# State-space pairs one turn later, and an out-projection that begins with the attention rows

## The chip, the cores and the metric

The kernel runs on one core of a Trainium2 chip. The metric is the device time of one execution in microseconds (us); the kernel before takes 3050.3 us (median of 3 runs, 3049.33 to 3051.59). The engines named here are TensorE (PE; PEld is its weight load), VectorE (DVE), ScalarE (ACT), GpSimd (POOL) and SyncE (SP), whose queue issues nearly all loads.

## The reference

One layer of a hybrid decoder over 512 prompt tokens and 8 sequences of 8 new tokens (576 columns). One projection feeds a sparse-attention group of 8 heads and a state-space (Mamba-2) group of 16 heads. Their outputs stand side by side and go through one output projection:

```python
u = rmsnorm(x, norm_attn)
proj = u @ w_in
q, k, v, qi, ki, wi, z, xbc, dtr = jnp.split(proj, _split_points(), axis=-1)
att = att_fn(q, k, v, qi, wi, ki)
y, h_fin = ssd_scan(xs, dt, A, Bm, Cm, h0, chunk)
y = (y + d_skip.astype(jnp.float32)[:, None] * xs.astype(jnp.float32)).astype(x.dtype)
y = rmsnorm(y.reshape(B, T, SSM_WIDTH) * jax.nn.silu(z), ssm_norm)
h = x + jnp.concatenate([att, y], axis=-1) @ w_out
f = rmsnorm(h, norm_ffn)
h = h + (jax.nn.silu(f @ w_gate) * (f @ w_up)) @ w_down
```

Two facts matter. The norm over `y` needs all 16 state-space heads, so no `y` row can be used before the last pair of heads has added its squares. The attention rows need no such norm.

## The kernel before, in words

Every large product is done in split precision: a weight block is cast to a high part (ACT, `WH`), the rest is its low part (POOL, `WL`), and TensorE adds three products, high by high, high by low, low by high. A half unit (`half_unit`, L802) is 8 input rows of 128, each 6 matmuls of 288 columns. Two half units make one output tile of 128 rows by 576 columns; inside the turns each half unit is called a product, numbered 0 to 5 (q, q, k, k, v, v of one head). Its raw weights come in halves (`load_half`, L480, tile `raw3`), three buffers deep.

After the conv stage come nine turns (`turn_pe`, `turn_act`, `turn_dve`, `turn_sp`). Turn i holds, interleaved by hand on every engine:

- `units`: products 0 to 5 of head i (turns 0 to 7). In turn 0 products 0 to 3 run first, in a row.
- `att`: the attention of head i - 1 (turns 1 to 8): logits of the prompt (L968), cached keys transposed (L987) and multiplied (L997), softmax, values (L1188), cached values (L1165), and a last transpose (L1169) before head i - 1 is stored to the DRAM tensor `mixS`.
- `mamba`: the state-space pair i (turns 0 to 7): transposes of x and B (L977), C by B (L1066), states per chunk (L1079), old states transposed (L1006), outputs per chunk (L1014, L1017), outputs of the new tokens (L1025), state update (L1175). Its inputs are eleven loads (`load_mamba`, L508 to L516), the last of them the old states `h0`. All of it waits on one semaphore, `ssm_in`. `load_mamba(i + 1)` goes out in turn i, after the states of pair i are stored (`hout`), because it overwrites the same tiles.

A PSUM bank of the turns is handed on by a count (`nth`), so the number of uses of each bank per turn is part of the program.

After turn 7 the squares of all pairs are summed (L1199), ACT takes the root (L1586), DVE the reciprocal (L2170). Turn 8 has only the attention of head 7. Then comes the output projection: 16 units over 16 rows of `mixS` that are loaded one by one into six buffers (`load_mix`, L607), the `y` rows scaled by DVE (`y_norm`, L2179), cast by ACT (L1611, `AH`), and their low part made by DVE (L2184, `AL`). Unit 0 takes each row as its low part is ready, in the order y rows 0 to 7 (rows 8 to 15 of `mixS`), then attention rows 0 to 7; the 15 units behind it find all rows in place. On SP, the first weights of `w_out` and the rows stand behind waits, the first being for `hout` of the last pair: the weights' buffer overlaps `h0`.

Of the kernel before, what the change touches and what calls it, by code (L numbers as in the profile page):

```python
# [13 lines left out]
P = 128  # L14
# [22 lines left out]
def build(nc, I, O):  # L37
    ctx = ExitStack()
    with ctx:
# [257 lines left out]
        MAMBA = {"xtok0", "xtok1", "btok0", "btok1", "cb0", "cb1", "su", "hTb0", "hTb1", "y0", "y1", "y2", "y3", "ys", "us0", "us1", "fin"}  # L297
        where = dict(turn)
        in_turn, in_mamba, in_att = {}, {}, {}
        n_all, n_mamba, n_att = [0] * 4, [0] * 4, [0] * 4  # L300
        for name, b in turn:
            in_turn[name] = n_all[b]
            n_all[b] += 1
            if name in MAMBA:
                in_mamba[name] = n_mamba[b]
                n_mamba[b] += 1
            else:
                in_att[name] = n_att[b]
                n_att[b] += 1

        def nth(name, i):

            b = where[name]
            if isinstance(i, int) and i == 0:
                return first[b] + in_mamba[name]
            if isinstance(i, int) and i == 8:
                return first[b] + n_mamba[b] + 7 * n_all[b] + extra[b] + in_att[name]
            return n_all[b] * i + (first[b] + n_mamba[b] - n_all[b] + in_turn[name])


        first, extra = list(count), [0, 0, 1, 1]
        for b in range(4):
            count[b] = first[b] + n_mamba[b] + 7 * n_all[b]
        plan("ssy0", 2)
        plan("ssy1", 3)
        for b in range(4):
            count[b] += n_att[b]
# [66 lines left out]
        def _(sp):  # L394
# [179 lines left out]
            turn_sp(7, mamba=False, more=False)  # L574
# [19 lines left out]
            def out_cols(q):  # L594

                def src(dst):
                    d = dst.rearrange("p (k c) -> p k c", c=256)
                    return [(d[:, 8 * h:8 * h + 8, :], wo_v[:, 8 - 8 * h:16 - 8 * h, 256 * q:256 * q + 256]) for h in range(2)]
                return src

            def load_mix(j):
# [205 lines left out]
        def _(pe):  # L807
# [201 lines left out]
            def y_chunk(i, c):  # L1009

                tclaim(pe, f"y{c}", i)
                pe.wait_ge(s["mt_done"], 10 * i + 2 * c + 2)
                for e in range(2):
                    last = mm(bank(f"y{c}")[e * DS:(e + 1) * DS, 0:P], xtok[:, c, e * DS:(e + 1) * DS], mt[:, (2 * c + e) % 4, :], start=True, stop=True)  # L1014
                if c:
                    pe.wait_ge(s["hT_done"], 4 * i + c)
# [3 lines left out]
            def y_decode(i):  # L1020
                tclaim(pe, "ys", i)
                pe.wait_ge(s["mt_done"], 10 * i + 10)
# [7 lines left out]
            def turn_pe(i, att=True, units=True, mamba=True):  # L1030
                a = i - 1
                early = isinstance(i, int) and i == 0
# [4 lines left out]
                if units:  # L1037
                    product(i, 0)
                    if early:
# [5 lines left out]
                        pe.wait_ge(s["h_init"], 4)  # L1045
# [8 lines left out]
                if mamba:  # L1054
                    pe.wait_ge(s["ssm_in"], LOADS * (i + 1))
# [17 lines left out]
                if mamba:  # L1073
                    tclaim(pe, "su", i)
                    pe.wait_ge(s["xw_done"], i + 1)
# [50 lines left out]
                def rest():  # L1126
# [13 lines left out]
                    if mamba:  # L1140
                        tclaim(pe, "fin", i)
                        pe.wait_ge(s["hT_done"], 4 * i + 4)
# [28 lines left out]
            def update(i, g):  # L1171

                tclaim(pe, f"us{g}", i)
                pe.wait_ge(s["bblk"], i + 1)
# [25 lines left out]
            turn_pe(8, units=False, mamba=False)  # L1200
# [81 lines left out]
        def _(act):  # L1282
# [171 lines left out]
            def exp_decay(i, n):  # L1454
                act.wait_ge(s["seg"], 10 * i + n + 1)
# [15 lines left out]
            def turn_act(i, att=True, units=True, mamba=True, nxt=True):  # L1471
                a = i - 1
                later = not (isinstance(i, int) and i == 0)
                latera = not (isinstance(i, int) and i <= 1)
                early = not later
# [7 lines left out]
                if mamba:  # L1483
                    act.wait_ge(s["ssm_in"], LOADS * (i + 1))
# [4 lines left out]
                    if later:  # L1489
                        act.wait_ge(s["xw_done"], i)  # L1490
# [6 lines left out]
                if mamba:  # L1497
                    if later:
                        act.wait_ge(s["bblk"], i)
# [44 lines left out]
                if att:  # L1544
# [3 lines left out]
                    for t in range(4):  # L1548
# [4 lines left out]
                        if t == 2 and mamba:  # L1553
                            if later:
                                act.wait_ge(s["finout"], 16 * i)
                            evac(i, "fin", fin, bank("fin")[:, 0:P])
                if mamba:
                    if not att:
                        if later:
                            act.wait_ge(s["finout"], 16 * i)  # L1560
                        evac(i, "fin", fin, bank("fin")[:, 0:P])
                    tgiven(act, "fin", i)
                    act.dma_start(bass.AP(O["ssm_prompt"].tensor, i * (P * P), [[P, P], [1, P]]), fin).then_inc(s["finout"], 16)
                    act.wait_ge(s["y_done"], i + 1)
                    act.dma_start(bass.AP(mixS.tensor, i * (P * NT) + 8 * P * NT, [[NT, P], [1, NT]]), xs[:, :]).then_inc(s["ymix"], 16)
                if att:
                    exp_logits(i, 4)
                if mamba:
                    act.wait_ge(s["h_done"], 2 * i + 2)
                    act.dma_start(bass.AP(O["ssm_sample"].tensor, i * (P * P), [[P, P], [NM * DS * P, NB], [1, P]]), h0[:, :, :]).then_inc(s["hout"], 16)  # L1570
# [8 lines left out]
            turn_act(0, att=False)  # L1579
# [3 lines left out]
            turn_act(7, nxt=False)  # L1583
            for h in range(2):
                wait(act, f"ssy{h}")
                taken(actv(rstd[:, h, :], bank(f"ssy{h}")[:, 0:HALF], ACT.Sqrt, bias=eps[:, :], scale=1.0 / (NM * DS)), f"ssy{h}")  # L1586
            turn_act(8, units=False, mamba=False)
# [854 lines left out]
```

## Time and profile before

| | |
|---|---|
| median of the runs | 3050.3 us (3049.33 to 3051.59) |
| profiled execution | 3047.6 us, of which the profiled span is 3045.6 us |
| TensorE busy | 2827.9 us (93%) |
| VectorE, ScalarE, GpSimd busy | 1509.6, 952.2, 548.0 us |
| mean granted TensorE clock | 0.965 of full |
| HBM traffic | 116 GB/s over the span |
| turn 0, from product 0 to 3 done to turn 1 | 540.4 to 597.0 us |
| turns 1 to 7 | 597.0 to 1150.9 us |
| turn 8 and the start of the output projection | 1150.9 to 1212.85 us |

Busy shares are averages over stages. Times of events are in us from the start of the span. The number in brackets at the end of a row of a timeline is how long the engine had been idle before it, and what ended that.

### The profile page before, as it was taken

Reading aid. Unit: us, or ns where it says so; the run is one execution under the profiler, and the core shown is the slowest. Engines: PE = TensorE matmul, PEld = TensorE weight load, DVE = VectorE, ACT = ScalarE, POOL = GpSimd, SP = SyncE. Lnnn points to the kernel's source line nnn. Section 1 sums busy time; section 2 is a strip of 40 time slices with the busy share of each in tenths; the row PEclk is TensorE's granted clock in tenths of the full one; section 3 lists DMA queues with packets and bytes.
Section 4 is the critical chain, followed back from the end, with each engine's and each line's share of the span. In section 5 each row is a group of like instructions: output and inputs, shape, how many; then the busy total and the mean of one; then the engine's idle time right before and its main releaser. Section 6 shows DMA issues by size and latency. Waiting matters only on the chain.

```text
span 3045.6 us, 49651 instructions
## 1 busy us (share of the span) xinstructions
PE 2827.9 (93%) x20713; PEld 2688.3 (88%) x20713; DVE 1509.6 (50%) x2311; ACT 952.2 (31%) x1442; POOL 548.0 (18%) x230
## 2 busy tenths in 40 slices
PE   6999999689999996997799999999999999999997
PEld 5887898577777773997799999999999999999997
DVE  3312599444444443213767667676766733222323
ACT  4223222133333322323443434334343322121222
POOL 1222233111111110332000000000000033333331
PEclk8999999799999997998899999999999999999999
DMA  6422231455555545433123233332323352323221
GB/s 201 119 67 77 68 106 50 126 145 145 152 148 152 151 139 169 140 127 104 64 94 124 99 119 100 108 112 97 127 99 107 127 198 99 114 99 115 99 99 63
DMA packets 367372, 354.00 MB, mean 116 GB/s; under 512 B 40957, under 2 KB 321125, under 8 KB 365880
## 3 DMA queue, kind: packets, MB, share of 16 engines
q1 hardware_dynamic: 334136, 325.20, 33.7%
q10 hardware_dynamic: 33024, 25.77, 2.6%
q8 instruction: 158, 2.59, 0.3%
q14 instruction: 54, 0.44, 0.0%
HBM read 303.18 MB, written 49.13 MB: 116 GB/s over the span
## 4 chain that ended last, share of the span: by engine, by line
PE 57%; issue 32%; POOL 7%; DVE 2%; ACTq 1%; ACT 1%; POOLq 0%; DVEq 0%
PE PS L1242 32%; PE PS L1224 18%; PE PS L802 6%; POOL WL L705 4%; POOL WL L734 3%; ACTq L1286 0%; DVE XR L2282 0%; ACTq L1287 0%; DVE xo_t L2287 0%; DVE xo_x L2287 0%; DVE y_out L2357 0%; POOL WL L726 0%; ACT WRAW L1295 0%; DVE rstd L2275 0%; PE PS L817 0%
## 5 line engine op out<-in xcount | busy, mean ns | idle before, releaser
L802 PE MATMUL PS<-AH,WH 128*128 128x288 f32 (+1 forms) x2208 | 493.5, 306 | 21.0 <-DVE AL L2184 7.3
L1224 PE MATMUL PS<-H,WH 128*128 128x288 f32 x2816 | 489.5, 296 | 0.7 <-DVE us L2249 0.7
L802 PE MATMUL PS<-AL,WH 128*128 128x288 f32 (+1 forms) x2208 | 481.1, 300 | 0.0
L802 PE MATMUL PS<-AH,WL 128*128 128x288 f32 (+1 forms) x2208 | 480.1, 299 | 0.0
L724 POOL TENSOR_TENSOR WL<-WRAW,WH 128x1024 fp32r<-128x1024 f32 x88 | 213.8, 2430 | 1378.8 <-ACT WH L717 1378.8
L1224 PEld LDWEIGHTS PS<-H,WH 128*128 128x128 f32 x2816 | 414.4, 189 | 0.9 <-issue 0.9
L802 PEld LDWEIGHTS PS<-AH,WH 128*128 128x128 f32 (+1 forms) x2208 | 363.6, 193 | 44.9 <-issue 28.9
L1242 PE MATMUL PS<-xo_t,WH 128*128 128x288 f32 x1888 | 380.1, 296 | 8.6 <-ACT kept L1643 7.5
L802 PEld LDWEIGHTS PS<-AL,WH 128*128 128x128 f32 (+1 forms) x2208 | 363.9, 193 | 0.0
L802 PEld LDWEIGHTS PS<-AH,WL 128*128 128x128 f32 (+1 forms) x2208 | 363.1, 192 | 0.0
L2343 DVE TENSOR_TENSOR XD<-PS,XD 128x576 f32<-128x576 f32 x176 | 133.4, 758 | 398.8 <-PE PS L1224 398.8
L1242 PEld LDWEIGHTS PS<-xo_t,WH 128*128 128x128 f32 x1888 | 303.6, 188 | 9.0 <-issue 9.0
L1224 PE MATMUL PS<-H,WL 128*128 128x288 f32 x1408 | 301.5, 296 | 0.0
L1242 PE MATMUL PS<-xo_x,WH 128*128 128x288 f32 x1408 | 285.4, 297 | 14.3 <-DVE xo_x L2287 14.3
L1242 PE MATMUL PS<-xo_t,WL 128*128 128x288 f32 x944 | 278.4, 295 | 0.0
L2200 DVE TENSOR_TENSOR WL<-WRAW,WH 128x1024 fp32r<-128x1024 f32 x147 | 179.9, 1224 | 126.8 <-ACT WH L1635 126.8
L1242 PEld LDWEIGHTS PS<-xo_x,WH 128*128 128x128 f32 x1408 | 227.7, 190 | 14.7 <-DVE xo_x L2287 14.7
L717 ACT CAST WH<-WRAW 128x1024 fp32r<-128x1024 f32 x88 | 92.7, 1054 | 435.5 <-PE PS L1224 430.7
L1224 PEld LDWEIGHTS PS<-H,WL 128*128 128x128 f32 x1408 | 226.9, 189 | 0.0
L1242 PE MATMUL PS<-xo_x,WL 128*128 128x288 f32 x704 | 208.3, 296 | 0.0
L1242 PE MATMUL PS<-xo_t,W 128*128 128x288 f32 x1392 | 196.0, 297 | 10.4 <-DVE xo_t L2287 10.4
L705 POOL TENSOR_TENSOR WL<-WRAW,WH 128x1024 fp32r<-128x1024 f32 (+1 forms) x58 | 139.4, 2406 | 361.3 <-ACT WH L700 361.3
(353 smaller groups left out, 3796.2 us busy)
## 6 DMA issues: line engine op xcount, KB each, us to landing
WRAW<-in_w_gate SPq DMA_DIRECT2D x22, 2048.0 KB
WRAW<-in_w_up SPq DMA_DIRECT2D x22, 2048.0 KB
WRAW<-in_w_down SPq DMA_DIRECT2D x22, 2048.0 KB
WRAW<-in_w_in SPq DMA_DIRECT2D x14, 2048.0 KB, 8.4
raw<-in_w_in SPq DMA_DIRECT2D x48, 512.0 KB, 4.1
kca<-in_cache_k SPq DMA_DIRECT2D x256, 64.0 KB, 2.8
vca<-in_cache_v SPq DMA_DIRECT2D x256, 64.0 KB, 2.0
WRAW<-in_w_out SPq DMA_DIRECT2D x16, 1024.0 KB
```

Of the source, the lines that this page charges most:

```text
L705: nc.gpsimd.tensor_tensor(WL[:, half, :, 0:w], raw[:, 8 * half:8 * half + 8, :], WH[:, half, :, 0:w].bitcast(F32), ALU.subtract).then_inc( ...
L717: nc.scalar.copy(as_down(WH, h % 2), w_down_half((1, 0)[f % 2], h)).then_inc(s["w_hi"], 1)
L724: nc.gpsimd.tensor_tensor(as_down(WL, h % 2), w_down_half((1, 0)[f % 2], h), as_down(WH, h % 2).bitcast(F32), ALU.subtract).then_inc(s["w_ ...
L734: nc.gpsimd.tensor_tensor(WL[:, half, :, :], raw, WH[:, half, :, :].bitcast(F32), ALU.subtract).then_inc(s["w_lo"], 1)
L802: last = nc.tensor.matmul(G[gslot][0:width, h, 0:HALF], wt[:, half, k % 8, 0:width], act[:, (k + shift) % KT, h * HALF:(h + 1) * HALF], st ...
L1224: last = mm(G[(slot + t) % 2][:, h, 0:HALF], wt[:, half, 2 * k + t, :], hid[:, m, k, h * HALF:(h + 1) * HALF], start=(k == 0 and wt is WH ...
L1242: last = mm(out, wt[:, k, :], act[:, m, k, :], start=(j in (0, 1, 3) and k == 0 and wt is wh and m == 0), stop=(k == 7 and wt is wl), skip ...
L2200: tt(w_low(r), operand(up, j, r), w_high(r).bitcast(F32), ALU.subtract).then_inc(s["p_lo"], 1)
L2343: tt(two(XD[:, n, :]), G[n % 2][:, :, 0:HALF], two(XD[:, n, :]), ALU.add).then_inc(s["tile_taken"], 1)
```

## The change

Pair i - 1 is now worked on in turn i, as attention head i - 1 is. Turn 0 holds only products, turn 8 holds head 7 and pair 7 together. The waits that count pairs go down by one pair each. The sum of squares, the root and the reciprocal come after turn 8, and the output projection takes the rows of `mixS` in their own order: attention rows 0 to 7, then y rows. On DVE the reciprocal now stands in the row loop, ahead of row 2. The two weight halves (0, 4) and (0, 5) are issued ahead of `load_mamba(0)`.

```diff
@@ load_mamba, SP @@
                     if n == 5 and mamba:
                         twait(sp, "ys", i)
-                        sp.wait_ge(s["ymix"], 16 * i + 16)
-                        sp.wait_ge(s["hout"], 16 * i + 16)
-                        sp.wait_ge(s["link_s"], 4 * i + 4)
-                        load_mamba(i + 1)
+                        sp.wait_ge(s["ymix"], 16 * i)
+                        sp.wait_ge(s["hout"], 16 * i)
+                        sp.wait_ge(s["link_s"], 4 * i)
+                        load_mamba(i)
...
-            load_mamba(0)
             load_half(0, 4)
             load_half(0, 5)
+            load_mamba(0)
             sp.wait_ge(s["w_lo"], 58)
...
-            turn_sp(0, att=False)
+            turn_sp(0, att=False, mamba=False)
...
-            turn_sp(7, mamba=False, more=False)
+            turn_sp(7, more=False)
             turn_sp(8, units=False, mamba=False)
...
-                if j == 15:
+                if j == 7:
                     sp.wait_ge(s["mixa"], 16 * NH)
-                sp.dma_start(mx[:, j % 6, :], mixS[(j + 8) % KT]).then_inc(mx_in[j % 6], 16)
+                sp.dma_start(mx[:, j % 6, :], mixS[j]).then_inc(mx_in[j % 6], 16)
@@ PE @@
-            turn_pe(0, att=False)
+            turn_pe(0, att=False, mamba=False)
             for i in range(1, 8):
                 turn_pe(i)
 
+            turn_pe(8, units=False)
             pe.wait_ge(s["link_s"], 4 * 8)
             pe.wait_ge(s["h_init"], 5)
...
-            turn_pe(8, units=False, mamba=False)
...
-                    half_unit(pe, C3 + 2 * n + h, h, (T3 + n) % 2, shift=8, ready=ready)
+                    half_unit(pe, C3 + 2 * n + h, h, (T3 + n) % 2, ready=ready)
@@ DVE @@
+            turn_dve(8, units=False)
             nc.vector.memset(ones[:, :], 1.0).then_inc(s["h_init"], 1)
-            for h in range(2):
-                given(dve, f"ssy{h}")
-            dve.wait_ge(s["tile_taken"], T3)
-            nc.vector.reciprocal(rstd[:, :, :], rstd[:, :, :]).then_inc(s["ry_done"], 1)
-            turn_dve(8, units=False, mamba=False)
...
-            y_norm(0)
-            y_norm(1)
             for j in range(KT):
+                if j == 2:
+                    for h in range(2):
+                        given(dve, f"ssy{h}")
+                    dve.wait_ge(s["tile_taken"], T3)
+                    nc.vector.reciprocal(rstd[:, :, :], rstd[:, :, :]).then_inc(s["ry_done"], 1)
                 dve.wait_ge(s["m_hi"], j + 1)
...
-                if j + 2 < 8:
+                if 8 <= j + 2 < KT:
+                    if j + 2 == 8:
+                        dve.wait_ge(s["ry_done"], 1)
                     y_norm(j + 2)
```

TensorE's queue at the end of turn 0 and the start of turn 1, before (`xs` and `bf` are x and B of pair 0, L1066 is C by B, L1006 the old states, L1014 and L1017 the outputs per chunk):

```order
L977 MATMUL PS<-ident,xs 128x128 x4
L979 MATMUL PS<-ident,xs 64x128
L977 MATMUL PS<-ident,bf 128x128 x4
L979 MATMUL PS<-ident,bf 64x128
L1066 MATMUL PS<-cf,bf 128x128 x4
L1069 MATMUL PS<-cf,bf 64x64
L1079 MATMUL PS<-xw,btok 128x128 x4
L1006 MATMUL PS<-ident,h_108 128x128 x4
L1014 MATMUL PS<-mt,xtok 64x128 x2
L1006 MATMUL PS<-ident,h_108 128x128 x4
L1014 MATMUL PS<-mt,xtok 64x128 x2
L1017 MATMUL PS<-cf,hT 128x128
```

These rows stood between product 3 and product 4. Now nothing does: product 4 follows product 3, product 5 follows it, and turn 1 begins.

TensorE's queue in turn 8 after the change, from the C by B products (L1054) to output chunk 1 (L1001, L1004); L974 are cached keys, L984 their logits, L993 the old states:

```order
L1054 MATMUL PS<-cf,bf 128x128 x4
L1057 MATMUL PS<-cf,bf 64x64
L974 MATMUL PS<-ident,kca 128x128 x8
L1067 MATMUL PS<-xw,btok 128x128 x4
L984 MATMUL PS<-kcaT,qpad 32x512 x2
L974 MATMUL PS<-ident,kca 128x128 x4
L993 MATMUL PS<-ident,h_108 128x128 x4
L974 MATMUL PS<-ident,kca 128x128 x4
L1001 MATMUL PS<-mt,xtok 64x128 x2
L984 MATMUL PS<-kcaT,qpad 32x512 x2
```

Before, turn 8 had only the rows with `kca` here; the others stand between them now, in the order that turns 1 to 7 already had, but without the products.

SP's queue at the end of the turns is in the same order in both; what changed is the event that its waits stand for. After:

```order
L579 DMA WRAW<-in_w_out 128x8x256 x2
L594 DMA mx<-mixS 128x576 x6
L579 DMA WRAW<-in_w_out 128x8x256 x2
L599 DMA xt<-xres 128x576 x2
L594 DMA mx<-mixS 128x576 x10
```

The first of these rows waits for the states of pair 7 to be stored (`hout`), which happened in turn 7 before and happens late in turn 8 now.

## Rows read from the trace of the kernel before

**Rows 1.** The page's chain that ended last, by line.

```profile
PE PS L1242 32%; PE PS L1224 18%; PE PS L802 6%; POOL WL L705 4%; POOL WL L734 3%; ACTq L1286 0%; DVE XR L2282 0%; ACTq L1287 0%; DVE xo_t L2287 0%; DVE xo_x L2287 0%; DVE y_out L2357 0%; POOL WL L726 0%; ACT WRAW L1295 0%; DVE rstd L2275 0%; PE PS L817 0%
```

**Rows 2.** Busy time by stretch, with granted clock (PEclk), DMA share and GB/s.

```profile
540.40:597.00 56.60, 33.65 (x179) 27.54 (x179) 22.73 (x60) 11.04 (x25) 7.02 (x3) 0.67 0.40 103
679.60:758.00 78.40, 72.95 (x544) 61.61 (x544) 36.40 (x88) 24.22 (x58) 14.21 (x6) 0.96 0.52 147
1151.00:1212.80 61.80, 35.28 (x178) 18.80 (x176) 17.61 (x36) 19.70 (x42) 3.06 (x2) 0.68 0.53 164
1165.00:1190.00 25.00, 17.01 (x57) 7.38 (x56) 0.78 (x3) 6.28 (x14) 0.00 (x0) 0.64 0.40 113
1190.00:1201.00 11.00, 5.98 (x37) 3.88 (x34) 2.42 (x5) 3.87 (x12) 0.00 (x0) 0.96 1.04 345
1206.40:1230.00 23.60, 15.28 (x82) 14.17 (x83) 19.56 (x26) 12.12 (x19) 5.19 (x2) 0.68 0.79 251
```

**Rows 3.** Timeline of TensorE in turn 0: start, length, what, idle before.

```profile
539.14 0.42 PE L802 MATMUL PS<-AH,WL 128*128 128x288 f32 x2
539.93 0.43 PE L802 MATMUL PS<-AH,WL 128*128 128x288 f32 x2
...
548.98 0.87 PE L977 MATMUL PS<-ident,xs 128*128 128x128 f32 x3 [8.62 <-issue]
...
574.04 0.83 PE L802 MATMUL PS<-AH,WH 128*128 128x288 f32 x2
...
597.02 0.92 PE L968 MATMUL PS<-kT,qT 128*128 128x128 f32 x4 [0.92 <-DVE vT L2012]
```

**Rows 4.** Timeline of SP in turn 0: the first state load, the weight halves.

```profile
536.33 0.43 SPq L508 DMA_DIRECT2D xs<-xcS  x1
...
542.27 4.70 SPq L480 DMA_DIRECT2D raw<-in_w_in  x2
```

**Rows 5.** TensorE's waits in turn 1, the longest: total, times, longest.

```profile
PE PS L977 <- DMA h<-in_state_ssm: 4.1, 1, 4.1
```

**Rows 6.** The page's DMA issues: size, median us to landing.

```profile
WRAW<-in_w_in SPq DMA_DIRECT2D x14, 2048.0 KB, 8.4
raw<-in_w_in SPq DMA_DIRECT2D x48, 512.0 KB, 4.1
```

**Rows 7.** Timeline of TensorE in turn 8.

```profile
1150.72 1.21 PE L1199 MATMUL PS<-ssq,ones 128*128 128x288 f32 x4
...
1157.83 3.36 PE L968 MATMUL PS<-kT,qT 128*128 128x384 f32 x4 [5.25 <-DVE lg L2019]
...
1196.42 1.13 PE L1188 MATMUL PS<-pt,vtok 128*128 128x128 f32 x8 [0.93 <-ACT pt L1442]
```

**Rows 8.** Timelines of ACT (two rows) and SP (last), end of turn 6.

```profile
1063.54 0.27 ACT L1442 COPY attT<-PS 128x128 f32<-128x128 f32 x1 [1.31 <-PE PS L1188]
...
1064.47 0.39 ACTq L1570 DMA_DIRECT2D ssm_sample<-h  x1
...
1068.16 0.33 SPq L508 DMA_DIRECT2D xs<-xcS  x1
```

**Rows 9.** Timeline of SP: the first weights of the output projection.

```profile
1189.73 1.21 SPq L592 DMA_DIRECT2D WRAW<-in_w_out  x2
```

**Rows 10.** Timeline of DVE: reciprocal, and rows of the output projection.

```profile
1153.79 3.75 DVE L2170 RECIPROCAL rstd<-rstd 128x576 f32<-128x576 f32 x1 [3.22 <-ACT rstd L1586]
...
1212.63 2.91 DVE L2179 SCALAR_TENSOR_TENSOR mx<-mx,gains,rstd 128x576 f32<-128x576 f32 x1
...
1217.53 0.81 DVE L2179 SCALAR_TENSOR_TENSOR mx<-mx,gains,rstd 128x576 f32<-128x576 f32 x1
...
1218.93 0.80 DVE L2179 SCALAR_TENSOR_TENSOR mx<-mx,gains,rstd 128x576 f32<-128x576 f32 x1
```

**Rows 11.** Timelines of ACT, then TensorE: unit 1 of the output projection.

```profile
1230.29 1.04 ACT L719 CAST WH<-WRAW 128x1024 fp32r<-128x1024 f32 x1
...
1233.92 0.51 PE L802 MATMUL PS<-AH,WH 128*128 128x288 f32 x2 [1.57 <-POOL WL L726]
```

More of the change, by code:

```diff
@@ L303, in build @@
             n_all[b] += 1
[L304 to L309, printed above, removed]
         def nth(name, i):
             b = where[name]
[L314 to L321, printed above, removed]
+            return first[b] + n_all[b] * (i - 1) + in_turn[name]
+        first = list(count)
         for b in range(4):
-            count[b] = first[b] + n_mamba[b] + 7 * n_all[b]
+            count[b] = first[b] + 8 * n_all[b]
         plan("ssy0", 2)
         plan("ssy1", 3)
-        for b in range(4):
-            count[b] += n_att[b]
         plan("ssf0", 2)
@@ L597, in src @@
                     d = dst.rearrange("p (k c) -> p k c", c=256)
-                    return [(d[:, 8 * h:8 * h + 8, :], wo_v[:, 8 - 8 * h:16 - 8 * h, 256 * q:256 * q + 256]) for h in range(2)]
+                    return [(d[:, 8 * h:8 * h + 8, :], wo_v[:, 8 * h:8 * h + 8, 256 * q:256 * q + 256]) for h in range(2)]
                 return src
@@ L1021, in y_decode @@
                 tclaim(pe, "ys", i)
[L1022 removed]
+                pe.wait_ge(s["mt_done"], 10 * i)
                 tgiven(pe, "hTb1", i)
@@ L1031, in turn_pe @@
                 a = i - 1
-                early = isinstance(i, int) and i == 0
+                early = i == 0
+                if i == 1:
+                    pe.wait_ge(s["h_init"], 4)
                 if att:
@@ L1472, in turn_act @@
                 a = i - 1
-                later = not (isinstance(i, int) and i == 0)
-                latera = not (isinstance(i, int) and i <= 1)
-                early = not later
+                later = i > 1
+                latera = i > 1
+                early = i == 0
                 if units and not early:
@@ L1554, in turn_act @@
                             if later:
-                                act.wait_ge(s["finout"], 16 * i)
+                                act.wait_ge(s["finout"], 16 * a)
                             evac(i, "fin", fin, bank("fin")[:, 0:P])
                 if mamba:
[L1558 to L1561, printed above, removed]
                     tgiven(act, "fin", i)
-                    act.dma_start(bass.AP(O["ssm_prompt"].tensor, i * (P * P), [[P, P], [1, P]]), fin).then_inc(s["finout"], 16)
-                    act.wait_ge(s["y_done"], i + 1)
-                    act.dma_start(bass.AP(mixS.tensor, i * (P * NT) + 8 * P * NT, [[NT, P], [1, NT]]), xs[:, :]).then_inc(s["ymix"], 16)
+                    act.dma_start(bass.AP(O["ssm_prompt"].tensor, a * (P * P), [[P, P], [1, P]]), fin).then_inc(s["finout"], 16)
+                    act.wait_ge(s["y_done"], i)
+                    act.dma_start(bass.AP(mixS.tensor, a * (P * NT) + 8 * P * NT, [[NT, P], [1, NT]]), xs[:, :]).then_inc(s["ymix"], 16)
                 if att:
@@ L1583, in _ @@
             turn_act(7, nxt=False)
+            turn_act(8, units=False)
             for h in range(2):
@@ L1606, in _ @@
                 act.wait_ge(mx_in[j % 6], 16 * (j // 6 + 1))
-                if j < 8:
-                    act.wait_ge(s["y_norm"], j + 1)
+                if j >= 8:
+                    act.wait_ge(s["y_norm"], j - 7)
                 if j == 0:
                     act.wait_ge(s["w_used"], C3)
-                copy(AH[:, (j + 8) % KT, :], mx[:, j % 6, :]).then_inc(s["m_hi"], 1)
+                copy(AH[:, j, :], mx[:, j % 6, :]).then_inc(s["m_hi"], 1)
             def squares(n):
@@ L2093, in turn_dve @@
                     twait(dve, "cb0", i)
-                    if not (isinstance(i, int) and i == 0):
-                        dve.wait_ge(s["finout"], 16 * i)
+                    if a:
+                        dve.wait_ge(s["finout"], 16 * a)
                     ttaken(tt(cbm[:, 0:4, :], bank("cb0")[:, :].rearrange("p (c j) -> p c j", c=4), cmask[:, :].rearrange("p (c j) -> p c j", c=1).to_broadcast([P, 4, P]), ALU.mult), "cb0")
```

58 lines of the change are left out of this document (27 added, 31 removed).

## The prediction

> **What bounds the kernel now.** I read the page's chain first: by line it is nearly all TensorE matmuls, with the casts of weights for them [rows 1]. So the time is TensorE's work plus its gaps, and a change that leaves the matmuls alone can only move gaps. The busy time by stretch shows where gaps are: from the end of product 3 to turn 1 (540.4 to 597.0) TensorE is busy 33.65 of 56.60 us at a granted clock of 0.67; in turn 8 and after (1151.0 to 1212.8) it is busy 35.28 of 61.80 at 0.68; a turn between them with everything in it is busy 72.95 of 78.40 at 0.96 [rows 2]. In the first stretch pair 0 runs alone, in the last head 7 runs alone. The change empties the first and puts its kind of work into the last. Both ends are on TensorE's own path, since the products and the output projection follow in order. Turns 1 to 7 keep their content (a head, a pair, six products), only the pair's number changes, so I cost them at nothing apart from one wait in turn 1.
>
> **Term 1, turn 0.** Before: the last matmul of product 3 ends at 540.4 (539.93 + 0.43). TensorE is then idle 8.62 us until the pair's inputs are in, works through the chain of the pair, starts product 4 at 574.04, and reaches turn 1 at 597.02 [rows 3]. That is 56.7 us.
> After: product 4 needs its weights. Their halves were issued at 542.27, behind the eleven loads of the pair that began at 536.33 [rows 4]; now they are the first, so at 536.3, and land 4.1 us later at the median [rows 6], at 540.4. From the start of a cast to the matmuls that use its low part it took 3.63 us (1230.29 to 1233.92) [rows 11]: product 4 starts at 544.1. Six matmuls took 0.79 us (539.14 to 539.93) [rows 3], so a half unit of eight such rows takes 6.3; after the idle 3.7 us I give the first 0.7 more. Product 4 ends at 551.1, product 5 at 557.4, and with the 0.92 us wait for v [rows 3] and 0.1 for the last matmul's end, turn 1 starts at 558.4. What else stands in the way is DVE: its q must be taken before product 4, which waits only for DVE's set-up and for constants issued before 536.3. Gain: 597.0 - 558.4 = 38.6 us.
> In turn 1 TensorE waited 4.1 us for the pair's last load [rows 5]. That load now goes out some 20 us before it is needed, so this goes too. Term 1: 42.7, which I round to 42 for small slips in the loads of head 1. Bounds: if the halves land as late as the 8.4 us of the larger weight loads [rows 6], 4 less; nothing makes it much more. 38 to 43.
>
> **Term 2, turn 8.** It starts after turn 7, which by the times of before is at 1150.9, just behind the sum of squares that now moves behind it [rows 7]. Head 7 alone ran from 1151.9 (behind the 1.21 us of the sum of squares) to the last values matmul at 1197.5, and had waited 5.25 us for logits that stood behind DVE's reciprocal [rows 7]. That reciprocal leaves: 45.6 - 5.2 = 40.4 us.
> Pair 7 is added. Bound from below: nothing, if it fits into TensorE's idle time (25.00 - 17.01 = 8 us in 1165 to 1190 alone [rows 2]). Bound from above: its whole chain as it ran alone, 597.0 - 549.0 = 48.0 us, less the two products of 6.3 and 7.0 inside it: 34.7. In between stands its work: in 540.4 to 597.0 TensorE was busy 33.65 us [rows 2], less 13.3 of products, so about 20 us, mostly at half clock. Part of it hides in the waits of head 7 for cached keys and for DVE. I take 15. So the last values matmul ends at 1150.9 + 40.4 + 15 = 1206.3; ACT issues the store of the states 0.9 us after it starts to copy that result, and SP's next load behind such a store went out 3.7 us later (1064.47 to 1068.16) [rows 8]. States stored: 1211.5. Turn 8 then needs some 4 us more for the cached values, which this store does not wait for.
>
> **Term 3, the start of the output projection.** Before, its first weights were issued at 1189.73 [rows 9] and were long there. The change adds no wait here, but the old wait for `hout` now ends at 1211.5, and behind it on SP's queue stand the first weights, six rows of `mixS`, the second weights, two residual rows, and the ten other rows. The weights (2 MB) land 8.4 us after issue [rows 6]: 1220.4 with the issue itself. Cast and low part, 3.6 [rows 11]: unit 0 starts at 1224.0.
> Its rows are then paced by DVE. Rows 0 and 1: 2 x 0.74. Reciprocal 3.75 [rows 10], which nothing hides now. Rows 2 to 5: 4 x 0.74. Rows 6 to 13, each with the scaling of a y row: 1.40 from one to the next (1217.53 to 1218.93) [rows 10], 8 x 1.40 = 11.2. Rows 14 and 15: 1.5. Sum 20.9. While POOL makes the first two low parts, DVE is held up: one scaling took 2.91 instead of 0.80 at that point [rows 10]; I add 2.9. 23.8 from about 1223.3, so DVE's last row is done at 1247.1 and ACT's last copy 0.8 earlier, at 1246.3; unit 1 starts 3.63 later [rows 11], at 1249.9. Before it was 1233.92. Loss: 16.0 us for terms 2 and 3 together.
> Could the loads be later than DVE? Row 6 is the first load behind the second weights: 2048 + 6 x 288 + 2048 + 2 x 288 + 288 KB = 6.85 MB. At the 345 GB/s of the stretch with weights in flight [rows 2] that is 19.9 us, so 1231.4; DVE comes to it at about 1234. No wait; at the 251 GB/s of the stretch 1206.4 to 1230.0 [rows 2] it is 27 us and DVE waits 5. Bounds of terms 2 and 3: 1 (pair hidden) to 41 us (whole chain, slower loads).
>
> On DVE's hold-up the Trainium skill, "SBUF — State Buffer", section "SBUF: two separate sides", says that a GpSimd instruction and a VectorE instruction with two SBUF inputs take an exclusive lock on a shared port pair, so that one waits out the other. The 2.91 us row agrees. By the rule in full, both low parts of 2.4 us or so could hold DVE, and the 2.9 would be up to 5, and the loss 18.
>
> **Sum.** -42 + 16.0 = -26. The profiled execution is 3047.6 us (span 3045.6), so 3021.6; the median of the runs is 2.7 above it, so 3050.3 - 26 = 3024.3, say 3025.
>
> **Rivals.**
> A: the pair hides in turn 8. For it: TensorE is idle 26.5 of 61.8 us there [rows 2], and where work was thicker the clock was full (0.96 in 1190 to 1201, against 0.64 in 1165 to 1190 [rows 2]). Against: most idle pieces are shorter than the pair's round trips through ACT and DVE. Price: the pair costs 3 instead of 15: 3013. The Trainium skill, "TensorE: Matmul & The Clock Gate", section "HAM oscillation — how this bites in real kernels", ties the half clock to waits between short bursts; a fuller turn 8 would run at full rate more of the time, which speaks for A.
> B: the pair's chain does not overlap with head 7's, since all engines are in order and each wait of one holds up the other, at half clock. For it: in turn 0 the same order of instructions waited for ACT and DVE again and again. Against: in turns 1 to 7 the two run in each other's shadow. Price: 34.7 instead of 15: 3044.
> C, slower: the loads of the output projection. 9.5 MB (6.85 and nine more rows) must come after 1211.5, and before most of it was covered by turn 8. It decides if the last row lands so late that the loss passes 42, which is unit 1 at 1276, last load at about 1271: 60 us, or 158 GB/s. At the 113 GB/s of 1165 to 1190 [rows 2] it is 84 us, and the time 3050 + 24 = 3074. Against: in that stretch TensorE's order set what was asked for, not the DMA engines (share 0.40); the large loads ran at 345 and 251.
> D: the change doesn't do what it says: turn 0's gap comes back in turn 1, because pair 0's or head 1's loads crowd each other where they were spread out. In 540.4 to 597.0 the DMA engines were busy only 0.40 [rows 2], which speaks against it. If half of term 1 comes back, 3046, which is no change.
>
> **Chances.** Forecast (pair costs 9 to 21, loads keep up) 0.57, between 3016 and 3034. A 0.15, B 0.16, D 0.06, C 0.06. The range must leave out no more than two in ten: it takes in A and most of B, 3011 to 3042. A run of this kernel can tell about 0.2% (6 us) from no change. Faster by more than that: forecast, A, and nearly all of B, 0.87; same: D and a rest of B, 0.07; slower: C, 0.06.
>
> **What would show it.** Right: turn 1 begins near 558 with a single idle piece of about 4 us before product 4; no wait for `h` in turn 1; turns 1 to 7 of 78.4 us each; turn 8 of 60 to 70 us; SP issues the first weights of `w_out` at turn 8's end, not in its middle, and TensorE waits 5 to 12 us between the sum of squares and unit 0, then is paced by DVE, with the reciprocal ahead of row 2. Wrong, if turn 8 is about 50 us (A) or over 80 us (B); if ACT's casts of late rows wait for DMA more than for DVE (C); if turn 1 is longer than 80 us (D). In the new trace all later times shift by the same amount, about 42 us earlier from turn 1 on.

## The result, and the profile after

| | median | lowest to highest | ratio to the kernel before |
|---|---|---|---|
| before | 3050.95 us (4 runs) | 3049.33 to 3052.89 | |
| after | 3019.39 us (4 runs) | 3015.99 to 3024.53 | 0.9898, 95% interval 0.9881 to 0.9915 |
| after, once more | 3017.36 us (4 runs) | 3015.92 to 3019.27 | 0.9886, 0.9865 to 0.9907 |

The change makes the kernel 31.6 us (1.0%) faster; 3025 was predicted. The profiled execution of after is the slowest of its four (3024.53 us, span 3022.4). Its chain by line is still TensorE's [rows 1]:

```profile
PE PS L1230 32%; PE PS L1212 19%; PE PS L789 6%; POOL WL L692 4%; POOL WL L721 3%; ACTq L1274 0%; DVE XR L2264 0%; ACTq L1275 0%; DVE xo_t L2269 0%; DVE xo_x L2269 0%; DVE y_out L2339 0%; POOL WL L713 0%; ACT WRAW L1283 0%; DVE rstd L2257 0%; PE PS L804 0%
```

Busy time by stretch, as in [rows 2]: first TensorE, then the weight loads, DVE, ACT, POOL, the granted clock, the DMA share. The rows are the end of product 3 to turn 1, 78.4 us of turns 2 and 3, turn 8 to the last values matmul, from there to unit 0, and unit 0:

```profile
548.40:568.70 20.30, 15.53 (x98) 15.31 (x97) 1.60 (x3) 3.96 (x4) 7.07 (x3) 0.83 1.06 285
651.30:729.70 78.40, 71.90 (x548) 60.69 (x548) 37.16 (x92) 24.42 (x59) 14.37 (x7) 0.98 0.55 153
1119.40:1165.30 45.90, 35.35 (x183) 22.29 (x183) 26.70 (x82) 16.42 (x47) 0.00 (x0) 0.81 0.52 143
1165.30:1184.30 19.00, 8.41 (x80) 5.60 (x79) 3.58 (x9) 8.50 (x15) 3.12 (x2) 0.59 0.85 290
1184.30:1209.90 25.60, 18.81 (x97) 16.42 (x97) 22.51 (x25) 10.76 (x16) 4.62 (x3) 0.77 0.64 203
```

The first stretch was 56.6 us and is 20.3. Turn 2 begins at 648.41, so turn 1 is 79.7 us where it was 82.6 (597.02 to 679.64). Turns 2 to 6 take 78.2 to 78.7 us, turn 7 79.6. In turn 8 the head and the pair together take 45.9 us; in the kernel before the head alone took 45.7, of which 5.25 was the wait behind the reciprocal:

```profile
1151.80:1197.50 45.70, 28.01 (x101) 13.77 (x99) 13.00 (x27) 14.17 (x31) 0.00 (x0) 0.70 0.47 141
```

TensorE's timeline of after (start, length, what, idle before), which answers to [rows 3, 7, 11]:

```profile
548.01 0.42 PE L789 MATMUL PS<-AH,WL 128*128 128x288 f32 x2
552.31 0.58 PE L789 MATMUL PS<-AH,WH 128*128 128x288 f32 x1 [3.87 <-POOL WL L721]
...
568.68 0.89 PE L955 MATMUL PS<-kT,qT 128*128 128x128 f32 x4 [0.90 <-issue]
...
648.41 0.89 PE L955 MATMUL PS<-kT,qT 128*128 128x128 f32 x4 [0.39 <-ACT attT L1430]
...
1119.45 3.97 PE L955 MATMUL PS<-kT,qT 128*128 128x128 f32 x8 [0.39 <-ACT attT L1430]
...
1127.18 1.11 PE L964 MATMUL PS<-ident,xs 128*128 128x128 f32 x4 [2.11 <-DMA h<-in_state_ssm]
...
1164.20 1.13 PE L1176 MATMUL PS<-pt,vtok 128*128 128x128 f32 x8 [0.99 <-ACT pt L1430]
...
1176.28 2.15 PE L1188 MATMUL PS<-ssq,ones 128*128 128x288 f32 x4
1184.29 0.82 PE L789 MATMUL PS<-AH,WH 128*128 128x288 f32 x2 [5.86 <-DVE AL L2164]
...
1209.88 0.51 PE L789 MATMUL PS<-AH,WH 128*128 128x288 f32 x2 [1.64 <-POOL WL L713]
```

One piece of idle time, 3.87 us, stands before product 4. TensorE's longest waits in turn 1 no longer hold one for `h` [rows 5]. But turn 8 now has one: TensorE waits 2.11 us there for the last load of pair 7 (2.5 in the second execution). Turn 1's longest waits:

```profile
PE PS L1001 <- DVE xs L2038: 1.2, 1, 1.2
PE PS L1176 <- ACT pt L1430: 1.0, 1, 1.0
PE PS L955 <- issue: 0.9, 1, 0.9
```

SP's issues: the halves for products 4 and 5 ahead of the pair [rows 4], and the first weights of `w_out` behind the stored states [rows 8, 9]; between them ACT's store of the states:

```profile
544.46 1.05 SPq L467 DMA_DIRECT2D raw<-in_w_in  x2
545.55 1.23 SPq L495 DMA_DIRECT2D xs<-xcS  x1
...
1170.32 1.02 SPq L579 DMA_DIRECT2D WRAW<-in_w_out  x2
1171.52 3.72 SPq L594 DMA_DIRECT2D mx<-mixS  x6
```
```profile
1166.31 0.39 ACTq L1554 DMA_DIRECT2D ssm_sample<-h  x1
```

DVE at the start of the output projection [rows 10], then what ACT did ahead of it:

```profile
1182.65 4.34 DVE L2164 TENSOR_TENSOR AL<-mx,AH 128x576 fp32r<-128x576 f32 x2 [6.62 <-ACT AH L1595]
1186.91 3.74 DVE L2162 RECIPROCAL rstd<-rstd 128x576 f32<-128x576 f32 x1
1190.58 2.69 DVE L2164 TENSOR_TENSOR AL<-mx,AH 128x576 fp32r<-128x576 f32 x4
```
```profile
1180.06 1.99 ACT L706 CAST WH<-WRAW 128x1024 fp32r<-128x1024 f32 x2 [0.74 <-DMA WRAW<-in_w_out]
1181.95 4.00 ACT L1595 CAST AH<-mx 128x576 fp32r<-128x576 f32 x6
```

DVE waits 6.6 us for the first copies of rows, and then works without a gap of 1 us until its last row (1207.1): it paces unit 0.

**The sum, term by term.** From the end of product 3 to turn 1: 56.7 before, 20.3 after, -36.4. From there to turn 8 (in the kernel before, to the sum of squares ahead of it): 553.7 and 550.8, -2.9. From there to unit 1: 83.2 and 90.4, +7.2. Together -32.1. Behind unit 1 there are 1811.7 and 1812.5 us, +0.8. The two profiled spans differ by only 23.2, since in this execution of after product 3 ended at 548.4 instead of 540.4, in code that the change leaves alone (experiment 1 has the cause): -32.1 + 0.8 + 8.1 = -23.2.

### The profile page after: what moved, and what is told of

It reads as the page before. It is cut to its first block, busy times and chain, and to the rows that moved or that the text cites. A ratio compares the mean times of both kernels' runs of the same rounds, so it can differ in the third digit from the quotient of the medians.

```text
span 3022.4 us, 49649 instructions
## 1 busy us (share of the span) xinstructions
PE 2830.1 (94%) x20713; PEld 2694.1 (89%) x20713; DVE 1508.8 (50%) x2311; ACT 949.1 (31%) x1440; POOL 548.8 (18%) x230
## 4 chain that ended last, share of the span: by engine, by line
PE 57%; issue 31%; POOL 7%; DVE 2%; ACTq 1%; ACT 1%; POOLq 0%; DVEq 0%
PE PS L1230 32%; PE PS L1212 19%; PE PS L789 6%; POOL WL L692 4%; POOL WL L721 3%; ACTq L1274 0%; DVE XR L2264 0%; ACTq L1275 0%; DVE xo_t L2269 0%; DVE xo_x L2269 0%; DVE y_out L2339 0%; POOL WL L713 0%; ACT WRAW L1283 0%; DVE rstd L2257 0%; PE PS L804 0%
```

## The experiments

Eleven kernels ran, in three groups, each group beside the kernel before. The median of the kernel before was 3053.51 us in the first group (again, pair_loads_first, turn8_head_only, y_rows_first), 3047.95 in the second (before_halves_first, first_weights_early, rows_in_turn8, fillers_turn8) and 3050.23 in the third. So medians are compared within a group, and ratios across groups (0.001 is 3 us). Where two variants are compared, I take their traces from a named matmul to a named matmul, since the part up to the end of product 3 alone varies by up to 10 us. Each variant has one trace.

**1. The same kernel again.**

> The changed kernel unchanged, for a second profile. Its first profiled execution was 8.0 us later than the kernel before already at the end of product 3, in code that the change does not touch. Theory (chance: one execution out of several): the time is near 3019 and product 3 ends anywhere between 538 and 549. Rival (the change makes the early part slower, by where its instructions lie or by its semaphores): product 3 ends at 548 again, within 1 us.

3017.36 us, ratio 0.9886. In its profiled execution product 3 ended at 540.43:

```profile
544.24 0.82 PE L789 MATMUL PS<-AH,WH 128*128 128x288 f32 x2 [3.81 <-POOL WL L721]
...
560.50 0.68 PE L955 MATMUL PS<-kT,qT 128*128 128x128 f32 x3 [0.90 <-issue]
```

So the 8 us do not belong to the change. Of the 13 profiled executions eleven end product 3 at 538.8 to 541.7 us, and two at 548.4 and 548.5 (after and pair_loads_first). Just these two have a lower granted clock in two early stretches, 180 to 200 (0.83) and 340 to 360 (0.83 and 0.74), where the other eleven have 1.00. The busy time by stretch, again and then after:

```profile
180.00:200.00 20.00, 18.14 (x115) 14.88 (x115) 6.82 (x23) 6.51 (x11) 4.74 (x2) 1.00 0.37 112
```
```profile
180.00:200.00 20.00, 18.91 (x106) 15.89 (x105) 6.45 (x24) 4.81 (x8) 4.71 (x2) 0.83 0.37 111
```

ACT's casts of weights in after lag those of again by 0.44 us at 184, by 3.45 from 202 on and by 6.46 from 358 on. So each of the two stretches costs some 3 us; why the clock fell there is open, and so are the last 1.5 us. The span of again is 3013.8, 31.8 less than before, close to the difference of the medians; its three terms are -36.6, -4.3 and +8.0.

**2. The order of loads.**

```diff
-            load_half(0, 4)
-            load_half(0, 5)
             load_mamba(0)
+            load_half(0, 4)
+            load_half(0, 5)
```

> The changed kernel with the one order of loads undone: the eleven loads of pair 0 again ahead of the weight halves of products 4 and 5. Theory (the path through turn 0 is half issued, half landed, cast, product): the halves go out 6 us later, as in the kernel before (536.3 to 542.3), product 4 starts 6 us later and the time is 6 us above the changed kernel, 3025. Rival (the order does not matter, the gap before product 4 has another cause): 3019, and product 4 at the same distance from product 3 as in the changed kernel, 3.9 us.

3030.75 us (3024.65 to 3034.23), ratio 0.9925 (0.9907 to 0.9943): 13 us slower than the changed kernel by the medians. Its profiled execution is 15.0 us longer than that of again: 8.3 in turn 0 (28.4 us from the end of product 3 to turn 1 instead of 20.1), and 8.1 ahead of product 3, with the lower clock of experiment 1; later parts give back 1.4. So the order is priced at 8.3 by one pair of traces; the medians say up to 13. Its timelines of TensorE and of SP, and its busy time by stretch:

```profile
561.70 0.82 PE L789 MATMUL PS<-AH,WH 128*128 128x288 f32 x2 [13.22 <-POOL WL L721]
```
```profile
544.48 0.43 SPq L495 DMA_DIRECT2D xs<-xcS  x1
...
550.45 3.83 SPq L467 DMA_DIRECT2D raw<-in_w_in  x2
```
```profile
549.00:553.00 4.00, 0.00 (x0) 0.00 (x0) 0.27 (x1) 0.00 (x0) 0.00 (x0) 0.74 0.96 230
553.00:557.00 4.00, 0.00 (x0) 0.00 (x0) 0.00 (x0) 0.00 (x0) 0.00 (x0) 0.50 1.06 284
```

The issue is 6.0 us later as I expected, and the halves then take 7.6 us to ACT's cast (558.09) instead of 4.2, with all DMA engines busy (share 0.96 to 1.06) on the pair's loads, the halves and, from 554.5 on, cached keys. The theory held; its price was too low, because it priced only the issue.

**3. The same order of loads in the kernel before.**

> The kernel before with one thing of the change alone: the weight halves of products 4 and 5 are loaded ahead of pair 0's eleven inputs, and pair 0 stays in turn 0. Theory (the gain of turn 0 comes from taking the pair off the path, the order of loads only keeps it): TensorE still does pair 0 ahead of product 4, and its inputs come 1 to 5 us later, so 1 to 5 us slower than the kernel before in its first stretch, 3052 to 3056. Rival (the order of loads is what brought the gain): 15 us or more faster, 3035 or less.

3051.32 us, ratio 1.0007 (0.9999 to 1.0016), which is 2 us slower or none. The pair starts 2 us later and product 4 still comes 25.05 us behind it. Order alone gains nothing: the gain is the pair's leaving, and the order keeps the next wait from taking its place.

**4. Turn 8 with the head alone.** Pair 7 is left out, on all engines. With it go its load, SP's waits for its stored states and its uses of the PSUM banks, and the last row of `mixS`, which nobody writes, is replaced by the one before it:

```diff
-            turn_pe(8, units=False)
+            turn_pe(8, units=False, mamba=False)
```

> The changed kernel without pair 7: turn 8 has head 7 alone, pair 7 is not computed (its row of the output projection's input is another pair's). It prices the pair in turn 8 directly. Theory (the pair fits into the waits of head 7, costs 5 us there, and some 2 us more since the first weights of the output projection wait for its states): from turn 8's first matmul to the last values matmul 40.5 instead of 45.9 us, the time 7 to 8 us below the changed kernel, 3012. Rival 1 (the term as I predicted it, 15 us): 3004 or less. Rival 2 (the pair is wholly hidden and the loss at the output projection comes from the order of its rows): 3017 to 3019.

3007.78 us (3006.49 to 3009.66), ratio 0.9854: 9.6 below the changed kernel by the medians.

```profile
1149.70 1.13 PE L1182 MATMUL PS<-pt,vtok 128*128 128x128 f32 x8 [0.94 <-ACT pt L1436]
...
1193.08 0.51 PE L795 MATMUL PS<-AH,WH 128*128 128x288 f32 x2 [1.65 <-POOL WL L719]
```

Turn 8 began at 1110.6, so the last values matmul ends 40.2 us later, and unit 1 starts at 82.5. In the second execution of the changed kernel these are 46.7 and 91.2. So the pair costs 6.5 us in the turn and 8.7 us up to unit 1, the later first weights included. My 15 is out for these two executions, and by the medians (9.6 for all of it); so is a wholly hidden pair.

**5. The order of the rows.** The reciprocal moves ahead of all rows with it:

```diff
-                sp.dma_start(mx[:, j % 6, :], mixS[j]).then_inc(mx_in[j % 6], 16)
+                sp.dma_start(mx[:, j % 6, :], mixS[(j + 8) % KT]).then_inc(mx_in[j % 6], 16)
...
+            nc.vector.reciprocal(rstd[:, :, :], rstd[:, :, :]).then_inc(s["ry_done"], 1)
+            dve.wait_ge(s["ry_done"], 1)
+            y_norm(0)
+            y_norm(1)
             for j in range(KT):
-                if j == 2:
...
```

> The changed kernel with the state-space rows first in the output projection, as before the change, and the reciprocal ahead of them: it prices the order of the rows alone. Theory (DVE has the same 21 us of work for the sixteen rows in either order and paces unit 0, and the reciprocal only moves from behind row 1 to ahead of row 0, into a wait of DVE for the first copies): within 3 us of the changed kernel, 3016 to 3022. Rival (attention rows, which need no norm, let unit 0 start early, and that is worth the chain of sum, square root and reciprocal): 8 to 10 us slower, 3028.

3015.37 us (3012.36 to 3021.03), ratio 0.9880: no slower than the changed kernel. From the sum of squares to unit 1 it takes 30.2 us, where attention rows first take 33.6. DVE's timeline:

```profile
1174.29 3.75 DVE L2160 RECIPROCAL rstd<-rstd 128x576 f32<-128x576 f32 x1 [3.23 <-ACT rstd L1571]
1178.08 3.65 DVE L2156 SCALAR_TENSOR_TENSOR mx<-mx,gains,rstd 128x576 f32<-128x576 f32 x2
```

The reciprocal stands here in the time in which DVE otherwise waits for copies. The half of the change that reorders rows gains nothing, and by these traces it costs some 3 us; the intervals overlap. In this execution turn 8 took 51.7 us to its last values matmul, with the same instructions as 46.7; see experiment 8.

**6. First weights early.**

```diff
-            sp.wait_ge(s["hout"], 16 * 8)
-            load_w(0, out_cols(0), 0)
...
+            sp.dma_start(*first_w[0]).then_inc(s["w_first"], 16)
...
+            sp.wait_ge(s["hout"], 16 * 8)
+            sp.dma_start(*first_w[1]).then_inc(w_ld[0], 32)
```

> The changed kernel, with the first half of the output projection's first weights loaded without waiting for the stored states (its buffer is not theirs), the six rows next, and the second half behind the wait; ScalarE casts the first half, six rows, then the second half. Theory (the first copies of rows wait for 0.7 us of weights and 2.0 us of casts after the square root, and DVE then paces unit 0): unit 1 starts 33.6 - 1.7 = 32 us after the sum of squares, and the time is some 2 us below the changed kernel, 3015. Rival (the wait for the stored states is what the start of the output projection costs): 5 us or more below, 3012 or less.

3010.96 us (3008.68 to 3016.75), ratio 0.9872 (0.9854 to 0.9890). Unit 1 starts 29.8 us after the sum of squares, 3.8 less, not 1.7.

```profile
1172.91 3.11 DVE L2169 TENSOR_TENSOR AL<-mx,AH 128x576 fp32r<-128x576 f32 x2 [4.82 <-ACT AH L1600]
1175.94 3.74 DVE L2167 RECIPROCAL rstd<-rstd 128x576 f32<-128x576 f32 x1
```
```profile
1176.76 2.36 POOL L715 TENSOR_TENSOR WL<-WRAW,WH 128x1024 fp32r<-128x1024 f32 x1 [2.03 <-ACT WH L708]
```

DVE's first rows come 1.8 us sooner after the sum of squares, as expected. The other 2 us I had not foreseen: POOL's second low part now lies beside the reciprocal, which it does not hold up, and the first two rows take 3.11 instead of 4.34; DVE's wait at row 6 goes from 0.89 to 0.30. By the ratios the kernel is 4 us below again, between theory (2) and rival (5 or more).

**7. Rows inside turn 8.** ACT's copy of a row is `high_row`, DVE's subtraction `low_row`:

```diff
                     ttaken(copy(pt[:, 0, :], bank("pts")[:, :]), "pts")
+                    if i == 8:
+                        act.wait_ge(s["w_first"], 16)
+                        upper_p(act, C3, 0, 0, False)
+                        for j in range(6):
+                            high_row(j)
...
                 if att:
+                    if i == 8:
+                        for j in range(6):
+                            low_row(j)
                     twait(dve, "pvs", i)
```

> As first_weights_early, and the rows of heads 0 to 5 are loaded, copied by ScalarE and split by DVE inside turn 8, while both wait for the end of head 7 (7 us each between its probabilities and its last result); the ten other rows are loaded ahead of most of the second weights. Theory (DVE's 21 us of work for sixteen rows is what sets the start of unit 1, and 4.4 us of rows and all of the wait for the first copies can move into turn 8): unit 1 starts 22 to 24 us after the sum of squares instead of 33.6, and the time is 10 us below the changed kernel, 3007. Rival (the rows then stand in the way of head 7's end on ScalarE and DVE, or TensorE's own work of 12.6 us a unit at the low clock takes over): less than 5 us below, 3013 or more.

3011.28 us, ratio 0.9874: some 4 us below again by the ratios, not the 10 expected but less than 5, as the rival had it. Unit 1 starts 24.5 us after the sum of squares, but that comes 62.7 us after turn 8's start, not 57.6. DVE's timeline shows a part of it:

```profile
1166.87 5.79 DVE L2057 TENSOR_TENSOR AL<-mx,AH 128x576 fp32r<-128x576 f32 x6 [3.77 <-ACT AH L1470]
1172.59 0.34 DVE L2163 TENSOR_SCALAR attS<-PS,hmask 128x128 f32<-128x128 f32 x1
```

TensorE had finished head 7's last sums at 1170.6 and waited 3.03 us for DVE; the rest is a turn 8 of 49.3 us at a clock of 0.79. So the same idea once more, with the rows out of the way:

```diff
+                if i == 8:
+                    for j in range(3):
+                        high_row(j)
                 if att:
                     twait(act, "pts", i)
...
+                        for j in range(3, 6):
+                            high_row(j)
+                        act.wait_ge(s["w_first"], 32)
+                        upper_p(act, C3, 0, 0, False)
+                        actv(rstd[:, 0, 0:1], eps[:, :], ACT.Sqrt)
+                        high_row(6)
```

> As rows_in_turn8, mended by what its trace showed: three of the six rows are copied ahead of the wait for head 7's transposes; the cast of the first weights follows the rows (beside GpSimd's low part six rows had taken DVE 5.8 instead of 4.4 us); ScalarE loads the table of the square root inside turn 8 (1.28 us); three quarters of the first weights, all but the piece that shares the states' buffer, are loaded ahead of the wait; the second weights, which unit 1 does not need, come last. Theory (DVE's work on rows set the start of unit 1, and head 7's end was held up by rows only where they overlapped it): the sum of squares comes within 1 us of the changed kernel's (57.6 us after turn 8's first matmul, at the same clock), unit 1 starts 21 to 23 us behind it, and the time is 10 to 12 us below the changed kernel, 3006 to 3008 where the kernel before is at 3050. Rival (the work of rows competes with head 7 whatever the order): no better than rows_in_turn8, 8 us or less.

3006.76 us (3005.53 to 3009.45), ratio 0.9856 (0.9830 to 0.9882). The sum of squares stands at 58.7, unit 1 at 83.4 after turn 8's start (24.6 between): the first is 1.1 us from the changed kernel's 57.6, nearly as expected, and the second missed my 21 to 23, since DVE waited for row 7:

```profile
1177.93 0.76 DVE L2061 TENSOR_TENSOR AL<-mx,AH 128x576 fp32r<-128x576 f32 x1 [3.69 <-ACT AH L1470]
```

This is the best version by ratio: its four runs all lie below all eight of the changed kernel, and by the ratios it is 0.3 to 0.4% faster, though the intervals touch. Those of experiment 6 and of the first form overlap its interval too.

The third form moves one cast more (against the second form):

```diff
             for j in range(8, KT):
+                if j == 13:
+                    hi_p(C3 + 2, 2, 0)
                 high_row(j)
```

> As rows_in_turn8_b, and the cast of unit 1's first weights stands ahead of the last three rows instead of behind them. Theory (the 3.6 us from the last row to unit 1 are cast and low part, which now hide, but GpSimd's low part holds DVE up by some 2 us): 0 to 1.5 us below rows_in_turn8_b. Rival (the hold-up costs as much as it brings, or more): the same or up to 1 us above.

3010.30 us, ratio 0.9862 (0.9839 to 0.9884). DVE's timeline, then TensorE's, row 13 of unit 0 and the start of unit 1:

```profile
1189.30 2.92 DVE L2185 SCALAR_TENSOR_TENSOR mx<-mx,gains,rstd 128x576 f32<-128x576 f32 x1
```
```profile
1192.94 0.85 PE L794 MATMUL PS<-AH,WH 128*128 128x288 f32 x2 [2.44 <-DVE AL L2064]
...
1196.80 0.42 PE L794 MATMUL PS<-AH,WH 128*128 128x288 f32 x2
```

One scaling took 2.92 us beside POOL's low part of the moved cast. TensorE waited 2.44 us for the row behind it, and began that row and the next at the low clock (pairs of matmuls 0.48 us apart). Unit 1 then started without a wait, but 24.9 us after the sum of squares, where the second form has 24.6. So the trace has the rival: the hold-up costs as much as it brings. By the ratios the third form is 2 us above the second, in an execution with a turn 8 of 51.5 us; the intervals overlap, so the times decide nothing.

Last, the edits of experiments 5 and 6 together:

> y_rows_first and first_weights_early together. In the first, unit 1 started 30.2 us after the sum of squares, in the second 29.8, in the changed kernel 33.6. Theory (both shorten the same chain on DVE, where the reciprocal fills the wait for copies, and the two scalings took 3.65 us beside GpSimd's two low parts, of which one now comes later): 28 to 29 us, and the time within 2 us of first_weights_early. Rival (the two gains add up): 26 us, and 4 us below it.

3016.81 us (3010.23 to 3025.14), ratio 0.9890; 30.0 us from the sum of squares to unit 1, where experiment 6 alone has 29.8. Neither held: the scalings took 1.55 instead of 3.65, but one later took 2.92 beside POOL's other low part, and three of ACT's copies of late rows waited for their loads (0.37, 1.05 and 0.16 us). Moving that low part only moves the hold-up, unless it falls beside the reciprocal.

**8. Is the clock a cost of its own in turn 8?** Ahead of eleven places where TensorE may wait, such as:

```diff
+                    fill(i, 4)
                     kca_t(i, 2)
```

> The changed kernel with 44 matmuls of 128 x 128 (0.11 us each at the full clock) that nothing reads, in groups of four ahead of places in turn 8 at which TensorE waits. It asks whether the granted clock is a cost of its own there (0.81 from the turn's first matmul to the last values matmul). Theory (the pair cost only 6 us since it raised the clock; fuller still, the clock is near 1.0): the same stretch 2 to 4 us shorter than 46.7 us at a granted clock over 0.9, the time 3013 to 3016. Rival (the waits set the stretch, the clock does not matter): 0 to 5 us longer, 3017 to 3022, whatever clock is granted.

3020.82 us, ratio 0.9902, some 5 us above again by the ratios. Busy time up to the last values matmul, in four executions (fillers, again, y_rows_first, rows_in_turn8_c):

```profile
1109.70:1161.10 51.40, 43.38 (x271) 31.57 (x271) 27.02 (x82) 16.54 (x48) 0.00 (x0) 0.87 0.46 130
```
```profile
1109.80:1156.50 46.70, 35.59 (x183) 22.56 (x183) 27.12 (x82) 16.43 (x47) 0.00 (x0) 0.82 0.49 140
```
```profile
1108.60:1160.30 51.70, 39.99 (x183) 25.43 (x183) 27.13 (x82) 16.46 (x47) 0.00 (x0) 0.72 0.46 130
```
```profile
1108.50:1160.00 51.50, 39.90 (x183) 25.37 (x183) 27.13 (x82) 16.43 (x47) 0.00 (x0) 0.72 0.59 168
```

The last three have the same 183 matmul records. At 0.82 TensorE is busy 35.6 us and the stretch is 46.7; at 0.72 it is busy 39.9 and the stretch 51.6. Nearly all of the difference lies in the last quarter of the turn, where the same matmuls take longer, as the last values do in again and in y_rows_first:

```profile
1155.35 1.13 PE L1176 MATMUL PS<-pt,vtok 128*128 128x128 f32 x8 [1.00 <-ACT pt L1430]
```
```profile
1158.26 2.04 PE L1176 MATMUL PS<-pt,vtok 128*128 128x128 f32 x8 [0.99 <-ACT pt L1430]
```

So the clock is worth up to 5 us here, from one execution to the next; what decides it is open. But fillers do not buy it. In their one trace the clock is 0.87, higher than in any other, and the stretch is 4.7 us longer than in again: they added 7.8 us of busy time (the 44 matmuls have 88 records). The rival's number held, its reason (the clock does not matter) did not. With the head alone the clock did not matter: 0.70 in the kernel before and 0.79 in experiment 4, and 40.4 and 40.2 us.

## Why the prediction was right, and what was off

**Term 1, right in mechanism, 2 us too good.** Product 4 was predicted 3.7 us after product 3, and it started 3.9 and 3.8 us after. From there to turn 1 it took 16.4 us where I had 14.3: the eight rows of product 4 ran about half at the low clock (pairs of matmuls 0.48 us apart instead of 0.27 up to 549.2 in the second execution), and I had given 0.7 us for that. The wait for `h` in turn 1 (4.1) went, as said. Turns 1 to 7 came out 2.9 us shorter (4.3 in the second execution), and turn 1 alone 2.9 in both: 4.1 of the wait less, 1.2 of other time more. 36.4 + 2.9 = 39.3 (40.9) against 42.

**Term 2, the step "I take 15" was mis-sized.** The head alone was put at 40.4; head and pair took 45.9 and 46.7. So the pair cost 5.5 and 6.3, and 6.5 by experiment 4; in two executions of variants 11. My 15 started from 20 us of TensorE work as it stood in turn 0, at 0.67 of the clock. In turn 8, between experiment 4 and again, the pair added 9.7 us of busy time (25.89 to 35.59) at 0.79 and 0.82, half of my 20, and 3.2 of them went into idle time of the head's turn. TensorE also waits 2.1 to 2.5 us in turn 8 for pair 7's last load, which I had not looked for: I had only let that wait go in turn 1. How much of the cost it makes, no run shows. Rival A (a cost of 3) was nearer than my 15, and the cost lies outside the 9 to 21 that the forecast stood on, though the time fell into the forecast's own 3016 to 3034. Turn 8 was to last 60 to 70 us; up to the sum of squares it took 56.8 and 57.6. The reason of rival A is only half borne out. That the pair's chain, 34.7 us in turn 0, is mostly hidden in turn 8 is shown. That filling the turn raises the clock is not: the head alone had 0.70 in the kernel before and 0.79 in experiment 4, head and pair 0.72 to 0.82. The Trainium skill, "TensorE: Matmul & The Clock Gate", section "HAM oscillation — how this bites in real kernels", blames the low clock on waits between short bursts. The trace of the fillers agrees as far as the clock goes (0.87), but the stretch became longer. B is out: the pair's chain overlaps with the head's.

**The store of the states, right, by a slip.** From the last values matmul's end to SP's first weights I had 5.2 us; it was 5.0 (1165.3 to 1170.3). The two parts that I gave, 0.9 and 3.7, add up to 4.6 only.

**Term 3, right to 2 us.** First weights' issue to unit 0: 12.5 predicted, 14.0 measured. The weights took 9.7 us to ACT's cast, with the six rows in flight (DMA share 0.85), where I had 8.9 with the issue. From the cast to unit 0 it took 4.2 instead of 3.6, since unit 0 waited for DVE's first row, which POOL held up. Unit 0 to unit 1: 25.9 predicted, 25.6 measured, with the reciprocal ahead of row 2. The hold-up of DVE by POOL was put at 2.9; two rows took 4.34 instead of 1.49, which is 2.85. The loss of terms 2 and 3 was 7.2 (8.0 in the second execution) instead of 16.0: the pair took 9.5 less, the way from the first weights to unit 0 1.5 more, and small parts 0.8 less.

**Rivals.** C (loads of rows) is out: ACT's late rows wait for DVE (0.73 each), only rows 6 and 7 for DMA, which costs DVE 0.89 us. D (the gap comes back) is out: turn 1 is 79.7 us, under its 80.

Two sizes were off with opposite signs: term 1 brought 2.7 us less than predicted, terms 2 and 3 cost 8.8 less. Together they are the 6 us between 3025 and 3019.4. The path was right; that the total came so near is in part luck, since the pair was priced at more than twice its cost.

## What to carry to other kernels

When work moves from a thin stretch into another thin stretch, price it at most by the busy time it adds at the clock of the filled stretch (here 9.7 us, of which 6.5 were paid), not by what it took where it stood alone. Then look for the waits for its own inputs there. When a wait is removed, look at what is queued ahead of the next input: here the order in which loads were issued decided 8 us, though it was worth nothing before. Put an instruction that no neighbour holds up, as the reciprocal, beside the one that holds up others.

## What the runs showed of the hardware

- A POOL subtraction with two SBUF inputs (2.5 us) held up a DVE instruction with two SBUF inputs that started beside it: 2.92 us instead of 0.81 (rows_in_turn8_c). The reciprocal, with one, took 3.74 and 3.75 beside it (experiment 6, rows_in_turn8_b), and 3.75 without it. This is as the Trainium skill, "SBUF — State Buffer", section "SBUF: two separate sides", has it.
- The same instructions of turn 8 took 46.7 and 51.6 us in different executions, at a mean granted clock of 0.82 and 0.72. Early in the program, 180 to 200 and 340 to 360 us, two of 13 executions had a clock of 0.74 to 0.83 instead of 1.00, and lost some 3 us each time.
- A 512 KB load took 4.2 us from its issue to the cast that needed it, and 7.6 us behind eleven other loads, at a share of the DMA engines of 0.96 to 1.06.
